# Two transformer blocks on one core: down weights on semaphores of their own, unread products in waits, latent rope queries turned on VectorE, a smaller and later scratch fill

## The chip, the cores and the metric

The program runs on one core of one Trainium2 chip. The metric is the device time of one execution in microseconds (us); lower is better. TensorE multiplies matrices, VectorE and ScalarE work elementwise out of on-chip memory, GpSimd does slow vector work and issues gathers, SyncE only issues transfers. All matrices here are f32; a product of a 128x128 stationary block with 512 columns stands in the trace as two records.

## The reference, cut to what matters

Two blocks of two layers each work on 512 tokens of width 1024. In the first block, each layer has a latent attention (MLA, 8 heads) and a dilated attention:

```python
q = (rms_norm(c_q, q_norm_g) @ w_uq).reshape(B, S, MLA_HEADS, MLA_NOPE + MLA_ROPE)   # 384 -> 8 x (64 + 32)
q_rope = apply_rope(q[..., MLA_NOPE:], cos, sin)
s = (einsum('bqhd,bkhd->bhqk', qn, k_nope) + einsum('bqhr,bkr->bhqk', qr, k_rope)) * scale
```

apply_rope turns a pair of halves: (x1 cos - x2 sin, x1 sin + x2 cos). In the second block each layer ends in a mixture of 16 experts, of which each token takes two:

```python
for wg, wu, wd, cw in experts:          # wg, wu: 1024 x 256; wd: 256 x 1024
    acc += ((silu(t @ wg) * (t @ wu)) @ wd) * cw
```

## The kernel before, in words

There is no scheduler. Each engine has its instructions written out in order (functions marked on("tensor"), on("vector"), ...), and semaphores order the engines.

**Latent queries (first_block).** Events of the projection bank psA are numbered by hand: event n of a layer uses bank n % 2, and TensorE waits in bank_free(n) until event n - 2 has been copied out. PA_VM, PA_KM, PA_QM are the events of the values, the first keys and the first two queries, PA_MLA the first event of each pair of heads. For each head, w_uq holds 128 columns: 64 plain, 32 rope, and the same 32 rope columns with their halves swapped. So project_q makes one head of 128 rows with three products (384 inputs), and queries_out multiplies it by a table (scale, cos, sin) on VectorE. The scores multiply these 128 rows with keys whose rope rows stand twice, which adds the two parts of the rotation. Eight head projections are made per layer: two ahead of the first scores, and two in the second step (t = 1) of each of the pairs j = 0, 1, 2. A step (j, t) is: scores of one tile of queries, values of the step before, a projection, the transposition of the first head's probabilities, for some steps a further projection, the transposition of the second head's.

**Scratch fill.** ys in device memory receives the experts' outputs. GpSimd fills all of it once with finite numbers, at the end of first_block, and waits for it; VectorE waits for ys_filled before it sums the modulation columns.

**Experts (second_block).** Tokens are sorted into 12 runs of up to 128 rows (PARTS, RUNS). A run holds rows of one expert or of parts of two. USES is the order in which the 16 experts' weights are first used, EXP_BUFS = 5 buffers hold gate and up weights (gu_w) and down weights (down_w). SyncE issues the loads in load_experts. load_gate_up(u) waits until the gate product of the run that used the buffer before is done, load_down(u) until the down product of that run is. Both count on one semaphore, exp_loaded of the buffer, and weights(c), which TensorE runs ahead of gate_up(c), waits for 32 on it: for both. TensorE's order is turn_rows(c + 2), turn_hidden(c), gate_up(c + 1), down(c), and so on; the last run has its gate half (last_gate) and its up half (last_up) around down of the run before.

**Unread products.** unread(count) multiplies ones with ones into a bank that nobody reads. Before the change it stands at the program's start and in experts(l).

The parts of the second block that the change also touches: turn_ctx and the key and value projections of the context, route_turned and route (router logits, inside out_product), last_rows and second_rows (the sum of the experts' outputs over the tokens) and project_u (the odd layer's first projection).

## Time and profile before

| | us |
|---|---|
| median of 3 runs | 1970.52 (1969.63 to 1974.61) |
| the profiled execution, its own time | 1959.03 |
| its span | 1957.4 |
| TensorE busy | 1897.8 |
| VectorE, ScalarE, GpSimd busy | 750.1, 546.4, 732.5 |
| mean granted TensorE clock | 0.988 of 2.4 GHz |

Busy is the time in which an engine had an instruction at work. The granted clock is a share of 2.4 GHz; it takes the two levels 1.0 (2.4 GHz) and 0.5 (1.2 GHz), and a value between them is a mean over both. The profiled execution is 11.5 us below the median of the runs.

### The profile page before, as it was taken

What the parts mean: (1) busy time and instruction counts of PE and PEld (TensorE: products, weight loads), DVE (VectorE), ACT (ScalarE), POOL (GpSimd) and SP (SyncE); (2) the same over time, 40 slices, a digit from 0 to 9 for tenths busy, and PEclk for the clock granted to TensorE, in tenths of its full rate; (3) what the DMA queues carried; (4) which work ended last, traced back from release to release, by engine and by line L of the source; (5) the groups of instructions that cost most, each with busy time, mean ns of one, the idle gap of its engine ahead of it and who ended that gap; (6) DMA issues with size and microseconds to landing.
All of it is one profiled execution on the core that took longest, in us unless ns stands there. A gap on an engine that the chain in (4) does not pass through costs nothing.

```text
span 1957.4 us, 25950 instructions
## 1 busy us (share of the span) xinstructions
PE 1897.8 (97%) x9760; PEld 1005.7 (51%) x9760; DVE 750.1 (38%) x1637; ACT 546.4 (28%) x1187; POOL 732.5 (37%) x1065
## 2 busy tenths in 40 slices
PE   8999999999999999999999999999998899999988
PEld 6644556656457455565665455654443344444433
DVE  1343443433221243434336563843532401334424
ACT  3243432214321334422124222742211221012110
POOL 0767676765666667676700012100110100001101
PEclk9999999999999999999999999999999999999999
DMA  7332343244344353333384312042799722047996
GB/s 292 123 109 101 127 148 121 87 144 142 137 169 141 105 199 107 135 138 116 138 335 162 129 38 86 2 181 98 284 366 369 252 91 86 30 186 256 362 377 247
DMA packets 71706, 328.70 MB, mean 168 GB/s; under 512 B 8680, under 2 KB 11174, under 8 KB 56998
## 3 DMA queue, kind: packets, MB, share of 16 engines
q1 hardware_dynamic: 41688, 217.00, 29.9%
q0 software_dynamic: 26736, 98.58, 14.5%
q10 hardware_dynamic: 3168, 11.54, 1.5%
q8 instruction: 79, 1.29, 0.3%
q14 instruction: 35, 0.29, 0.0%
HBM read 288.29 MB, written 38.80 MB: 167 GB/s over the span
## 4 chain that ended last, share of the span: by engine, by line
PE 88%; DMA 5%; DVE 3%; issue 2%; ACT 1%; DVEq 1%; SPq 0%; POOL 0%; ACTq 0%; POOLq 0%
PE psA L464 26%; PE psA L1815 10%; PE psA L456 9%; PE psA L1950 6%; PE psA L1852 6%; PE psA L627 6%; PE psSO L1968 4%; PE psT L443 3%; DMA pool_mem<-in_w_dn 3%; PE psA L505 3%; PE psSO L534 3%; PE psSO L544 2%; DVE pool_mem L2894 1%; PE psSO L565 1%; PE psSO L600 1%
## 5 line engine op out<-in xcount | busy, mean ns | idle before, releaser
L464 PE MATMUL psA<-gB,pool_mem 128*128 128x512 f32 x1024 | 455.3, 597 | 0.0
L395 POOL TENSOR_TENSOR pool_mem<-pool_mem,cs 128x256 f32<-128x256 f32 x448 | 269.3, 634 | 126.4 <-DMA pool_mem<-in_mod_w 125.8
L464 PEld LDWEIGHTS psA<-gB,pool_mem 128*128 128x128 f32 x1024 | 189.5, 190 | 224.2 <-issue 224.2
L399 POOL TENSOR_TENSOR pool_mem<-pool_mem 128x256 f32<-128x256 f32 x336 | 248.1, 766 | 30.9 <-issue 22.9
L1815 PE MATMUL psA<-pool_mem 128*128 128x512 f32 (+1 forms) x528 | 210.7, 558 | 6.0 <-DVE pool_mem L1584 3.4
L456 PE MATMUL psA<-pool_mem,gB 128*128 128x256 f32 (+2 forms) x768 | 190.8, 404 | 1.7 <-ACT gB L797 1.2
L1764 POOL DMA_INDIRECT pool_mem<-xs_scratch,idx x38 | 35.4, 932 | 391.0 <-DVE idx L2568 361.1
L456 PEld LDWEIGHTS psA<-pool_mem,gB 128*128 128x128 f32 x768 | 144.6, 191 | 44.3 <-issue 8.3
L1950 PE MATMUL psA<-pool_mem 128*32 128x512 f32 (+1 forms) x896 | 146.2, 618 | 10.9 <-DMA pool_mem<-in_w_dn 10.9
L1815 PEld LDWEIGHTS psA<-pool_mem 128*128 128x128 f32 x528 | 100.3, 192 | 109.8 <-issue 99.8
L1852 PE MATMUL psA<-pool_mem 128*128 128x512 f32 x256 | 113.9, 595 | 0.8 <-issue 0.8
L627 PE MATMUL psA<-pool_mem 128*128 128x512 f32 x256 | 111.9, 594 | 0.0
L443 PEld LDWEIGHTS psT<-ident,pool_mem 128*128 128x128 f32 x624 | 74.3, 142 | 52.7 <-issue 45.3
L407 POOL DMA_DIRECT2D pool_mem<-in_mod_w x56 | 50.4, 904 | 129.8 <-issue 122.4
L1950 PEld LDWEIGHTS psA<-pool_mem 128*32 128x32 f32 (+1 forms) x896 | 48.6, 125 | 94.0 <-issue 94.0
L996 DVE LOAD_MASK_SELECT pool_mem<-psA x48 | 0.7, 14 | 243.8 <-PE psA L464 243.8
L443 PE MATMUL psT<-ident,pool_mem 128*128 128x128 f32 x624 | 89.0, 275 | 3.7 <-DVE pool_mem L975 1.9
L1968 PE MATMUL psSO<-pool_mem 128*32 128x512 f32 (+2 forms) x496 | 88.9, 609 | 1.0 <-DVE pool_mem L2687 1.0
L852 ACT ACTIVATE pool_mem<-pool_mem,rl 128x512 f32<-128x512 f32 x128 | 84.7, 710 | 7.7 <-DVE rl L1039 7.6
L816 ACT ACTIVATE pool_mem<-psA 128x256 f32<-128x256 f32 x32 | 12.3, 383 | 257.3 <-PE psA L456 257.3
L627 PEld LDWEIGHTS psA<-pool_mem 128*128 128x128 f32 x256 | 47.9, 190 | 58.4 <-issue 56.8
L1852 PEld LDWEIGHTS psA<-pool_mem 128*128 128x128 f32 x256 | 47.1, 190 | 55.0 <-issue 54.7
(345 smaller groups left out, 2371.0 us busy)
## 6 DMA issues: line engine op xcount, KB each, us to landing
pool_mem<-in_w_gu SPq DMA_DIRECT2D x32, 2048.0 KB, 13.8
pool_mem<-in_mod_w POOLq DMA_DIRECT2D x56, 1024.0 KB, 7.8
pool_mem<-in_w_dn SPq DMA_DIRECT2D x32, 1024.0 KB, 12.6
pool_mem<-in_w_qk SPq DMA_DIRECT2D x24, 1024.0 KB, 5.1
ys_scratch<-pool_mem POOLq DMA_DIRECT2D x1, 11264.0 KB, 42.1
ys_scratch<-pool_mem ACTq DMA_DIRECT2D x22, 512.0 KB, 11.5
pool_mem<-in_odd_w_in SPq DMA_DIRECT2D x5, 2048.0 KB, 9.7
pool_mem<-in_w_out SPq DMA_DIRECT2D x4, 2048.0 KB, 8.1
```

The source lines that it names most:

```text
L395: nc.gpsimd.tensor_tensor(wm[:, b, k], wm[:, b, k], c_all[:, k].to_broadcast([P, MCH]), ALU.mult)
L399: nc.gpsimd.tensor_tensor(wm[:, b, k], wm[:, b, k], wm[:, b, n + k], ALU.add)
L443: m = nc.tensor.transpose(psT[:, e % 2, tile(i)], block_in, ident[:])
L456: m = nc.tensor.matmul(psA[:, n % 2, 0:cols], hT[:, k, tile(t)], w[:, k, :], start=(k == 0), stop=(k == KD - 1))
L464: m = nc.tensor.matmul(psA[:, n % 2, :], w(i), src[:, k, :], start=(i == 0), stop=(i == len(ks) - 1))
L505: m = nc.tensor.matmul(psA[32 * t:32 * t + 32, n % 2, 0:2 * P], around(hT_wide[:, k, :])[:, c, t], near_w[:, k, :], start=(k == 0), stop=( ...
L627: m = nc.tensor.matmul(psA[:, half, :], mixT[:, k, tile(t)], width(OUT_SLOT[half], 512)[:, k, :], start=(k == 0), stop=(k == KD - 1))
L852: nc.scalar.activation(prob[:, h, 0:keys], prob[:, h, 0:keys], ACT.Copy, scale=rl[:, h:h + 1]).then_inc(p_normed, 1)
L1815: m = nc.tensor.matmul(psA[:, n % 2, 0:width], lhs, rhs, start=(i == 0), stop=(i == len(pairs) - 1))
L1852: m = nc.tensor.matmul(psA[:, half, :], mixT[:, k, tile(t)], halves[half][0][:, k, :], start=(k == 0), stop=(k == KD - 1))
L1950: m = nc.tensor.matmul(psA[lo:hi, b, :], xgT[:, b, k, lo:hi], gu_w[USES.index(r) % EXP_BUFS][:, k, :], start=(k == 0), stop=(k == KD - 1))
L1968: m = nc.tensor.matmul(psO[lo:hi, half, :], hidT[:, b, k * P + lo:k * P + hi], down_w[USES.index(r) % EXP_BUFS][:, k, half * 512:half * 51 ...
```

## The change

Six edits:

1. **Latent queries.** w_uq has 768 columns: the 64 plain columns of all heads (blocks 0 to 3, two heads each), then the 32 rope columns of all heads (blocks 4 and 5, four heads each). Six projections per layer are made in place of eight. VectorE scales the plain rows into qT (queries_out), and makes the rotation (turning_out): a shuffle that swaps halves, two multiplications by tables, and one addition of 32 rows for each head. qT is set to zero once, since its other 32 rows are now unused. Heads 6 and 7 are put in place later (turning_late).
2. **Order ahead of the first scores.** The rope block, the keys and the first plain block are projected first, the values (PA_VM) last.
3. **Down weights apart.** Gate and up weights count on gate_up_loaded, down weights on down_loaded (three semaphores, taken in turn). gate_up waits for the former, down for the latter. From expert u = 5 on, the load of gate and up is issued ahead of the down load of the expert before it. A down load also waits until the down load three before it has landed.
4. **Unread products** in eight more places of the code, and a larger count in an old one.
5. **Scratch fill.** Only the rows from ROWS[-1] on are filled (11 blocks of 128 in place of 22), by GpSimd behind its pooling work in the second block, from a tile of h. VectorE waits for it in add_output of layer 0.
6. The tables and the weight layout on the host side follow from 1.

```diff
-PA, PA_CKV, PA_V0, PA_VM, PA_KM, PA_QM, PA_GB, PA_OUT = 88, 4, 8, 16, 20, 21, 76, 80
-PA_MLA = (23, 29, 35, 41)
+PA, PA_CKV, PA_V0, PA_QR, PA_KM, PA_QM, PA_VM, PA_GB, PA_OUT = 86, 4, 8, 16, 17, 18, 19, 74, 78
+PA_MLA = (23, 28, 34, 39)
+PA_SECOND = (3, 4, 3)
...
-                load(0, d["w_uq"][L], 3 * 1024)
+                load(0, d["w_uq"][L], 3 * 768)
...
-            pool.wait_ge(const_loaded, 48)
-            ys = d["ys"].rearrange("(c p) n -> p c n", p=P)
-            pool.dma_start(ys, qtab[:].rearrange("p (o h) n -> p o (h n)", o=1).to_broadcast(list(ys.shape))).then_inc(ys_filled, 16)
-            pool.wait_ge(ys_filled, 16)
...
             turn_h(0, 1)
+            unread(6)
             turn_h(0, 2)
...
+                pe.wait_ge(w_loaded[0], 16 * (LOADS[0] * L + 2))
+                project_q(L, 4, PA_QR)
                 pe.wait_ge(spare_loaded, 48 * L + 32)
+                project_k(L, 0, PA_KM)
+                project_q(L, 0, PA_QM)
                 for t in range(NT):
                     n = PA * L + PA_VM + t
...
-                project_k(L, 0, PA_KM)
-                pe.wait_ge(w_loaded[0], 16 * (LOADS[0] * L + 2))
-                for h in range(2):
-                    project_q(L, h, PA_QM + h)
                 pe.wait_ge(*turned_of(TT * L + T_KR))
-                for t in range(NT):
-                    pe.wait_ge(*copied_of(PA * L + PA_VM + t))
...
-                                project_q(L, 2 * j + 2, n + 2)
+                                project_q(L, 5 if j == 1 else j + 1, n + 2)
...
-                            elif t == 1:
-                                project_q(L, 2 * j + 3, n + 3)
+                            elif t == 1 and j == 1:
+                                project_q(L, 2, n + 3)
...
-            def queries_out(L, head, n):
+            def queries_out(L, j, n):
                 n += PA * L
                 dve.wait_ge(pa_ready, n + 1)
-                nc.vector.tensor_tensor(qT[:, (head // 2) % 2, head % 2, :], psA[:, n % 2, :], qtab[:, head % 2, :], ALU.mult)\
-                    .then_inc(pa_copied[n % 2], 1)
+                for h in range(2):
+                    m = nc.vector.tensor_scalar(qT[rows(h), j % 2, h, :], psA[rows(h), n % 2, :], QK_M ** -0.5, None, ALU.mult)
+                m.then_inc(pa_copied[n % 2], 1)
+
+            def turning_out(L, block, n):
+                n += PA * L
+                dve.drain()
+                dve.wait_ge(pa_ready, n + 1)
+                nc.vector.stream_shuffle(swapped[:], psA[:, n % 2, :], MIRROR)
+                nc.vector.tensor_tensor(turning, psA[:, n % 2, :], qtab[:, 0, :], ALU.mult).then_inc(pa_copied[n % 2], 1)
+                dve.drain()
+                nc.vector.tensor_tensor(swapped[:], swapped[:], qtab[:, 1, :], ALU.mult)
+                dve.drain()
+                for head in range(4 * block, 4 * block + (2 if block else 4)):
+                    out, own = turning_rows(head)
+                    nc.vector.tensor_tensor(out, turning[own], swapped[own], ALU.add)
+                if block:
+                    nc.vector.tensor_tensor(turning[rows(1)], turning[rows(1)], swapped[rows(1)], ALU.add)
+                    dve.drain()
...
             def load_down(l, u, e):
                 b = u % EXP_BUFS
                 if u >= EXP_BUFS:
                     sp.wait_ge(yc_half[1], RUNS * l + RUN_OF[USES[u - EXP_BUFS]] + 1)
-                sp.dma_start(down_w[b], rows(d["w_dn"][l][e])).then_inc(exp_loaded[b], 16)
+                if l or u >= DOWN_SEMS:
+                    sp.wait_ge(down_loaded[u % DOWN_SEMS], DOWN_LOADED[u % DOWN_SEMS] * l + 16 * (u // DOWN_SEMS))
+                sp.dma_start(down_w[b], rows(d["w_dn"][l][e])).then_inc(down_loaded[u % DOWN_SEMS], 16)
...
+                behind = None
                 for u in range(EARLY + 1, EXPERTS):
                     e = expert_of(u)
                     load_gate_up(l, u, e)
-                    load_down(l, u, e)
+                    if behind:
+                        load_down(l, *behind)
+                    behind = (u, e)
+                load_down(l, *behind)
...
+            unwritten = d["ys"][ROWS[-1]:, :].rearrange("(c p) n -> p c n", p=P)
+            pool.dma_start(unwritten, h[:, 0:1, :].to_broadcast(list(unwritten.shape))).then_inc(ys_filled, 16)
...
+            def keep_warm(bank, count):
+                for _ in range(count):
+                    nc.tensor.matmul(bank[:, 0:P], ones[:], ones[:], start=True, stop=True)
...
                 route(l, 2)
+                keep_warm(psA[:, 0, :], 3)
                 turn_residual(3, 1)
+                keep_warm(psA[:, 0, :], 5)
                 route_turned(l, 3)
+                keep_warm(psA[:, 0, :], 1)
                 route(l, 3)
...
-                unread((0, 1)[l])
+                unread((2, 1)[l])
...
                 def down(c):
                     b = c % 2
+                    down_weights(c)
...
                 if l == 0:
+                    keep_warm(psA[:, 0, :], 6)
                     second_rows(1)
...
+            keep_warm(psO[:, 1, :], 8)
             pe.wait_ge(t_copied, T_K)
...
             turn_tile(T_ODD, N_ODD, 2)
+            keep_warm(psS[:, 0, :], 5)
             project_u(2)
             turn_tile(T_ODD, N_ODD, 3)
+            keep_warm(psS[:, 0, :], 5)
             project_u(3)
```

How this moves instructions, at three places. First TensorE in layer 0 of the first block, the steps (j = 0, t = 1) and the scores of the next, before (L464 is a projection's product, L443 a transposition, L534 scores, L544 values):

```order
L534 MATMUL psSO<-pool_mem 128x512 x2
L544 MATMUL psSO<-pool_mem 64x128 x8
L464 MATMUL psA<-pool_mem 128x512 x3
L443 MATMUL psT<-ident,pool_mem 128x128 x4
L464 MATMUL psA<-pool_mem 128x512 x3
L443 MATMUL psT<-ident,pool_mem 128x128 x4
```

and now (L532, L542, L462, L441 are the same lines of the changed kernel):

```order
L532 MATMUL psSO<-pool_mem 128x512 x2
L542 MATMUL psSO<-pool_mem 64x128 x8
L462 MATMUL psA<-pool_mem 128x512 x3
L441 MATMUL psT<-ident,pool_mem 128x128 x8
L532 MATMUL psSO<-pool_mem 128x512 x2
```

The second projection between the two transpositions is gone; the same holds for j = 2, and for both layers, four places in all.

Second, SyncE's loads in layer 0 of the experts, from expert u = 4 on, before (L1629 loads gate and up weights, L1635 down weights; an ISA row carries the wait of the load behind it):

```order
L1629 DMA pool_mem<-in_w_gu 128x4096
L1635 ISA
L1635 DMA pool_mem<-in_w_dn 128x2048
L1520 TENSOR_LOAD plan
L1520 ISA x2
L1629 ISA [waits gu_ready]
L1629 DMA pool_mem<-in_w_gu 128x4096
L1635 ISA [waits yc_half1]
L1635 DMA pool_mem<-in_w_dn 128x2048
```

and now (L1660 gate and up, L1668 down):

```order
L1660 DMA pool_mem<-in_w_gu 128x4096
L1551 TENSOR_LOAD plan
L1551 ISA x2
L1660 ISA [waits gu_ready]
L1660 DMA pool_mem<-in_w_gu 128x4096
L1668 ISA [waits down_loaded1]
L1668 DMA pool_mem<-in_w_dn 128x2048
L1551 TENSOR_LOAD plan
L1551 ISA x2
L1660 ISA [waits gu_ready]
L1660 DMA pool_mem<-in_w_gu 128x4096
L1668 ISA [waits down_loaded2,yc_half1]
```

Each down load now stands one place later, behind the gate and up load of the next expert.

Third, TensorE at the end of the router of layer 0 before (L1835 and L1829 are logits, L1542 a transposition, L1878 and L1882 rows of gates that are needed later):

```order
L1835 MATMUL psSO<-pool_mem 128x20
L1542 MATMUL psT<-ident,pool_mem 128x128 x4
L1829 MATMUL psSO<-pool_mem,rtw 32x128 x8
L1835 MATMUL psSO<-pool_mem 128x20
L1878 MATMUL psA<-gB,ones 128x512
```

and now (L1878, L1573, L1872 and L1924 are those lines, L1862 the unread products):

```order
L1878 MATMUL psSO<-pool_mem 128x20
L1862 MATMUL psA<-ones 128x128 x3
L1573 MATMUL psT<-ident,pool_mem 128x128 x4
L1862 MATMUL psA<-ones 128x128 x5
L1872 MATMUL psSO<-pool_mem,rtw 32x128 x8
L1862 MATMUL psA<-ones 128x128
L1878 MATMUL psSO<-pool_mem 128x20
L1924 MATMUL psA<-gB,ones 128x512
```

Nine unread products stand ahead of three instructions that wait for VectorE or ScalarE.

## Rows read from the trace of the kernel before

**Rows 1.** The page's part 1: busy us, share of the span, instructions.

```profile
PE 1897.8 (97%) x9760; PEld 1005.7 (51%) x9760; DVE 750.1 (38%) x1637; ACT 546.4 (28%) x1187; POOL 732.5 (37%) x1065
```

**Rows 2.** TensorE's waits: us in total, times, longest us.

```profile
PE psA L1950 <- DMA pool_mem<-in_w_dn: 10.9, 2, 5.8
PE psA L1986 <- DMA pool_mem<-in_w_dn: 4.8, 2, 2.4
PE psT L1924 <- DMA pool_mem<-xs_scratch,idx: 4.0, 2, 2.8
PE psSO L2072 <- DMA pool_mem<-ys_scratch,slots: 2.5, 1, 2.5
...
PE psA L1815 <- DVE pool_mem L2432: 2.3, 1, 2.3
PE psT L443 <- DVE pool_mem L975: 1.9, 1, 1.9
PE psSO L534 <- DVE pool_mem L1027: 1.8, 2, 0.9
```

**Rows 3.** Timeline of TensorE, step (j = 0, t = 1): start us, us.

```profile
117.67 2.74 PE L464 MATMUL psA<-pool_mem 128*128 128x512 f32 x6
...
120.25 0.60 PE L443 MATMUL psT<-ident,pool_mem 128*128 128x128 f32 x4
```

**Rows 4.** Timeline of VectorE and ScalarE, layer 0 of the first block.

```profile
78.71 2.80 DVE L1107 COPY pool_mem<-psT 64x512 f32<-64x512 f32 x4
...
115.04 1.32 ACT L852 ACTIVATE pool_mem<-pool_mem,rl 128x512 f32<-128x512 f32 x2
...
115.25 3.08 DVE L1127 CAST pool_mem<-pool_mem 128x512 bf16<-128x512 f32 x4
```

**Rows 5.** Timeline of TensorE, last runs of layer 0's experts.

```profile
1492.23 9.17 PE L1950 MATMUL psA<-pool_mem 128*32 128x512 f32 x64 [5.18 <-DMA pool_mem<-in_w_dn]
...
1506.00 7.07 PE L1950 MATMUL psA<-pool_mem 128*32 128x512 f32 x64
...
1520.23 5.34 PE L1968 MATMUL psSO<-pool_mem 128*32 128x512 f32 x32
```

**Rows 6.** The same, layer 1.

```profile
1896.70 10.02 PE L1950 MATMUL psA<-pool_mem 128*32 128x512 f32 x64 [5.77 <-DMA pool_mem<-in_w_dn]
```

**Rows 7.** Stretches: us, TensorE busy (records), granted clock, DMA share, GB/s.

```profile
18.50:22.00 3.50, 3.50 (x11) 0.51 1.05 441
1175.60:1179.10 3.50, 3.50 (x10) 0.51 0.00 0
1363.40:1370.20 6.80, 6.21 (x24) 0.50 0.99 363
1380.40:1387.30 6.90, 6.25 (x14) 0.51 0.48 156
1545.10:1548.60 3.50, 3.50 (x6) 0.63 1.01 399
1405.00:1487.00 82.00, 82.00 (x510) 1.00 0.99 359
1500.00:1510.00 10.00, 10.00 (x98) 1.00 0.73 267
```

**Rows 8.** The chain that ended last: start us, us; transfers of down weights.

```profile
1474.46 17.63 DMA pool_mem<-in_w_dn
...
1506.63 12.46 DMA pool_mem<-in_w_dn
```

**Rows 9.** The page's part 6: transfers, KB each, us to landing.

```profile
pool_mem<-in_w_dn SPq DMA_DIRECT2D x32, 1024.0 KB, 12.6
...
ys_scratch<-pool_mem POOLq DMA_DIRECT2D x1, 11264.0 KB, 42.1
```

**Rows 10.** Timeline: GpSimd's last pooling instruction, VectorE ahead of add_output.

```profile
1231.51 1.27 POOL L1745 TENSOR_TENSOR pool_mem<-pool_mem 128x512 f32<-128x512 f32 x1
...
1295.21 0.18 DVE L2447 TENSOR_TENSOR pool_mem<-ident 128x20 f32<-128x20 f32 x1 [3.81 <-PE psSO L2172]
```

More of the change, by code:

```diff
@@ L121, in first_block @@
     t1, t2 = swapped[:, 0:256], swapped[:, 256:512]
+    turning = at(W_AT + 19200, S)
+    MIRROR = list(range(ROPE_M // 2, ROPE_M)) + list(range(ROPE_M // 2))
     SWAP = list(range(ROT_D // 2, ROT_D)) + list(range(ROT_D // 2)) + list(range(ROT_D, 32))
@@ L510, in project_k, with project_q @@
                 columns(PA * L + n, lambda k: ukv_v[k][:, tile(j)], cT, (3, 4))
-            def project_q(L, head, n):
-                columns(PA * L + n, lambda k: uq_v[:, k, tile(head)], cT, (0, 1, 2))
+            def project_q(L, block, n):
+                columns(PA * L + n, lambda k: uq_v[:, k, tile(block)], cT, (0, 1, 2))
             def project_ga(L, j, n):
@@ L549, in mla_values @@
             def mla_values(L, m):
+                for t in range(NT if m == 0 else 0):
+                    pe.wait_ge(*copied_of(PA * L + PA_VM + t))
                 for h in range(2):
@@ L1022, in dil_turned_out, with turning_rows, turning_late @@
                     .then_inc(turned_copied[e % 2], 1)
-            def queries_out(L, head, n):
+            def queries_out(L, j, n):
                 n += PA * L
                 dve.wait_ge(pa_ready, n + 1)
-                nc.vector.tensor_tensor(qT[:, (head // 2) % 2, head % 2, :], psA[:, n % 2, :], qtab[:, head % 2, :], ALU.mult)\
-                    .then_inc(pa_copied[n % 2], 1)
+                for h in range(2):
+                    m = nc.vector.tensor_scalar(qT[rows(h), j % 2, h, :], psA[rows(h), n % 2, :], QK_M ** -0.5, None, ALU.mult)
+                m.then_inc(pa_copied[n % 2], 1)
+            def turning_rows(head):
+                start = HD * (1 - head % 2)
+                return qT[start:start + ROPE_M, (head // 2) % 2, head % 2, :], slice(ROPE_M * (head % 4), ROPE_M * (head % 4) + ROPE_M)
+            def turning_out(L, block, n):
[13 more added lines that the diff above has]
+                    dve.drain()
+            def turning_late():
+                for head in (6, 7):
+                    out, own = turning_rows(head)
+                    nc.vector.tensor_copy(out, turning[own])
             def gated_out(L, k, gate, n):
@@ L1108, in _ @@
                 m.then_inc(turned_copied[e % 2], 1)
-                for h in range(2):
-                    queries_out(L, h, PA_QM + h)
+                turning_out(L, 0, PA_QR)
+                queries_out(L, 0, PA_QM)
                 for j in range(PAIRS_1):
@@ L1129, in _ @@
                             queries_keys_out(L, 0, j, t // 2)
-                        elif j < 3 and t == 1:
-                            queries_out(L, 2 * j + 2, n + 2)
                         elif j == 3 and t != 2:
@@ L1136, in _ @@
                             rotated(0, j, t // 2)
+                        elif j == 1 and t == 1:
+                            turning_out(L, 1, n + 2)
+                            queries_out(L, 2, n + 3)
                         elif j < 3 and t == 1:
-                            queries_out(L, 2 * j + 3, n + 3)
+                            if j == 2:
+                                turning_late()
+                            queries_out(L, j + 1, n + 2)
                         elif j == 3 and t != 2:
@@ L1276 @@
 MOVES = sum(1 for parts in PARTS for r, _, _, _ in parts if r >= STATIC)
-LOADED = [32 * len(USES[b::EXP_BUFS]) for b in range(EXP_BUFS)]
+LOADED = [16 * len(USES[b::EXP_BUFS]) for b in range(EXP_BUFS)]
+DOWN_SEMS = 3
+DOWN_LOADED = [16 * len(USES[b::DOWN_SEMS]) for b in range(DOWN_SEMS)]
 GATHERED = [16 * sum(len(parts) for parts in PARTS[b::2]) for b in range(2)]
@@ L1460, in second_block @@
     y2_added = sem("y2_added")
+    ys_filled = sem("ys_filled")
     r_ready = sem("r_ready")
@@ L1481, in per_layer @@
         return [sem(f"{name}{l}") for l in range(DEPTH)]
-    exp_loaded = [sem(f"exp_loaded{b}") for b in range(EXP_BUFS)]
+    gate_up_loaded = [sem(f"gate_up_loaded{b}") for b in range(EXP_BUFS)]
+    down_loaded = [sem(f"down_loaded{b}") for b in range(DOWN_SEMS)]
     idx_moved = sem("idx_moved")
@@ L3072, in layouts @@
     out["mask"] = -8 * mask
-    out["q_tab"] = np.stack([np.concatenate([plain, turned]), np.concatenate([turned, plain])], 1).astype(np.float32)
+    out["q_tab"] = np.concatenate([turned] * 4).astype(np.float32)
     return {k: np.ascontiguousarray(v) for k, v in out.items()}
```

50 lines of the change are left out of this document (25 added, 25 removed).

## Prediction

> **What bounds the kernel now.** I read the page's first part, then the table of waits, then the timeline of the stages that the change touches, then the granted clock over short stretches. TensorE is busy for 97% of the span [rows 1], so time can be won in three ways only: less work on TensorE, shorter waits of TensorE, and work that runs at 2.4 instead of 1.2 GHz. The table of waits shows that no single wait is long; the largest are the two for down weights ahead of the gate product L1950 (10.9 us in two waits) and ahead of the last gate product L1986 (4.8 us in two) [rows 2]. The stretches show the third part: in some places the granted clock is 0.50 or 0.51, the lower of its two levels, while TensorE is busy nearly throughout [rows 7]. Work that runs there takes twice as long. A difference of about 0.3% (6 us) is what a measurement of this kernel can tell from no change.
>
> **Edit 1, two projections fewer per layer.** A head's projection is six records, and lasts from 117.67 to 120.25 us, 2.58 us [rows 3]. Two go per layer, over two layers four: 4 x 2.58 = 10.3 us. All of it is on the path, because TensorE had no wait in these steps. Does one come up? In the shortened step, the second transposition moves from 120.25 to about 117.7. It needs the second head's probabilities, which ScalarE finished at 115.04 + 1.32 = 116.36 [rows 4], 1.3 us before. The values of this step need VectorE's copy of the first head's transposition. In layer 0 the mask casts end at 115.25 + 3.08 = 118.3 [rows 4], and that copy (0.7 us) now stands directly behind them, so it ends at 119.0, while TensorE wants it behind the transposition (0.6 us) and the next scores (four records at 0.43): at 117.7 + 0.6 + 1.7 = 120.0. So I charge nothing.
>
> VectorE gets more work. Copies of 64 rows took 2.80 / 4 = 0.70 us each [rows 4], as much as full ones, so the 32-row additions are priced alike. turning_out is then 7 instructions for block 4 and 6 for block 5, some 4.9 and 4.2 us. Block 5 comes at j = 1, t = 1; with the two instructions of queries_out behind it, VectorE comes about 2 us late to the maximum of the next scores. That next step (t = 2) has a full projection of 7 us between scores and transposition, which covers it. If that cover were gone it would cost 2 us per layer. The other end of this price is nothing.
>
> **Edit 2, the order ahead of the first scores.** The first scores waited 0.9 us per layer for the last query to be copied, 1.8 us in total [rows 2]. Four value products (1.7 us each, four records) now stand between that copy and the scores: the wait goes. A smaller one comes: counted from the end of the rope block's projection, turning_out holds VectorE for 4.9 us and the copy of the first plain block needs 1.4 more, 6.3; the keys (1.7), the plain block (2.6) and the first value product (1.7) fill TensorE for 6.0, and the second value product needs that bank. I charge 0.3 us per layer (bounds: nothing, and 1.4 us if all of the copy shows). Edits 1 and 2 together: 10.3 + 1.8 - 0.6 = **11.5 us**.
>
> **Edit 3, down weights apart.** The gate product at 1492.23 had waited 5.18 us and then took 9.17 us, against 7.07 us for the next one of the same shape: 2.1 us more [rows 5], since the wait had brought the clock down. In layer 1 the wait is 5.77 us and the product 10.02 us, 2.95 us more [rows 6]. The last gate product waited 4.8 us in both layers together [rows 2], and the down product behind it took 5.34 us in layer 0 for 32 records, where half of 7.07 is 3.5: 1.8 us [rows 5]. In all 10.9 + 4.8 + 2.1 + 2.95 + 1.8 = 22.5 us.
>
> What stands in its place? The transfers run at 359 GB/s with a share of 0.99 from 1405 to 1487 us [rows 7]: the stage is limited by bandwidth, and a new order makes no bytes go away. But the first gate product to wait (run 9) needs gate and up weights up to u = 12, and waited for the down weights of u = 12, landed at 1474.46 + 17.63 = 1492.1 [rows 8]. In the new order the down loads of u = 11 and 12 stand behind that gate and up load: 2 x 1.05 MB less [rows 9], at 359 GB/s 5.8 us, so it lands at 1486.3. TensorE comes at 1492.23 - 5.18 = 1487.05: no wait, by little. From there to the gate and up weights of u = 15 the queue holds the same bytes as between the two down loads of before, which landed at 1492.1 and 1519.1 [rows 8]: 27 us, and 2.7 us of it lay idle (share 0.73 over 10 us, [rows 7]) because a down load waited for its buffer at the queue's head. So they land between 1486.3 + 27 = 1513.3 and 1510.6. TensorE would reach the last gate product 5.2 + 2.1 us before 1516.7 (1519.1 less a wait of 2.4), at 1509.4. The wait is then 1.2 to 3.9 us; the DMA also has idle time to use around 1400 us, which the new order uses, so it may be nothing. I take 1 us per layer: 22.5 - 2 = **20.5 us**. Down weights are waited for in down(c), 8 us after the gate product begins; a landing that is 5.8 us later than the gate and up weights' is covered. The new wait of a down load for the one three before it is harmless while a load lands in 12.6 us [rows 9], since three loads are issued over two runs, and a run takes 7.07 + 3.5 = 10.6 us or more.
>
> **Edit 4, unread products.** Each has a quarter of the columns of one product of a projection, 2.58 / 3 / 4 = 0.21 us. At each place they are shorter than the wait that they stand in: 6 (1.3 us) in 1.9 us at the start, 8 (1.7) in 2.3 ahead of the context's projection, 2 of full width (1.7) in 2.8 ahead of L1924, 6 (1.3) in 2.5 ahead of L2072 [rows 2]. They cost nothing there; were none covered, all 48 narrow and 2 wide ones would cost 12 us. What they give back is time at the lower level [rows 7]: half of 3.5 us at 18.5 us and again at 1175.6 us, 1.75 us each; at 1380.4 half of 6.25 us, 3.1 us; at 1545.1 (1 - 0.63) x 3.5 = 1.3 us. In the 6.8 us from 1363.4 TensorE is behind VectorE's routing for most of the time, so that I count 1.0 of 3.1 us. Sum **8.9 us**; the bounds are -12 and +11. I take the full value, because each fill lies in the wait just ahead of a slow stretch.
>
> The Trainium skill, "TensorE: Matmul & The Clock Gate", section "Part 1: The HAM clock gate", says that the clock's monitor runs freely and doesn't begin anew with the kernel's work, so that the place of a change of clock shifts from run to run. By that rule a fill may stand where no fall would have come, and a fall come where no fill stands. If half of the 8.9 us were lost so, the sum would be lower by 4.5 us.
>
> **Edit 5, the scratch fill.** 11264 KB landed in 42.1 us [rows 9], hidden under TensorE's work; half of it takes about 21 us. GpSimd can issue it at 1231.51 + 1.27 = 1232.8, and VectorE asks for it at 1295.2 [rows 10]: 62 us later, hidden again. Nothing either way; if it were late, the first output product's bank would wait, 1 us for each us.
>
> **Sum.** 11.5 + 20.5 + 8.9 = 40.9 us off the span of 1957.4, which gives 1916.5, and 1918.1 for that execution's own time of 1959.03. The median of the runs is 11.5 us above it; I take the same difference off it: 1970.5 - 40.9 = 1929.6.
>
> **The rivals.**
> - *The clock falls anyway.* The fills leave waits of 0.2 to 1 us, and short gaps were enough before. Then the 8.9 us are gone: 1938.5. By the skill's rule above, part of this is to be expected. Chance 0.2.
> - *The wait for weights only moves on.* The stage's bandwidth bounds it; at a slightly lower rate than in the profile, the last gate product waits 6 to 8 us per layer and brings the clock down again. Then edit 3 gives about 8 us instead of 20.5: 1942. For it speaks the DMA share of 0.99; against it the 2.7 us that lay idle. Chance 0.17. Both together: 1951, chance 0.06.
> - *More than forecast.* The timed runs are 11.5 us above the profiled one; if that is in the waits for weights, edit 3 takes part of it too: 1920. Chance 0.06.
> - *Slower.* Down loads stand behind a gate and up load that waits for a buffer. If each down load so landed after its down product was due, each of the 11 runs behind the first would wait for one load, 1.05 MB at 359 GB/s = 2.9 us, over two layers 64 us; against 20 us from the other edits it is slower by 44, 2014. It decides from the point at which a down load is issued less than its landing time, 13 us, ahead of its product. Now that is 24 us or more (it may be issued once the run of five experts before is done), so it gets 0.03.
> - *It does nothing,* because the new waits eat up the gains: 1970, chance 0.02.
>
> **How the numbers follow.** The forecast has 0.46, with a range of its own of 1923 to 1936. The range of 1917 to 1948 takes in the first two rivals and the case of a larger gain, and leaves out the double rival, the slower one and no change, with the tails some 0.17. Faster by over 0.3%: all but the last two, 0.95. Within 0.3%: 0.02. Slower: 0.03.
>
> **What the profile of the changed kernel would show.** Edit 1: 24 projection records fewer (four projections of six), and a second transposition directly behind the first at t = 1. Edit 2: no wait of the scores at L534's place. Edit 3: no wait ahead of the gate product of run 9, and one of at most 4 us ahead of the last gate product, now for gate and up weights. Edit 4: a granted clock of 1.00 in the five stretches of rows 7 that show less, and a mean clock near 0.998. Edit 5: one transfer of 5632 KB at about 1233 us. The prediction is wrong if the wait of the last gate product is over 5 us, if the clock still falls at the router, or if a new wait comes in the attention's steps.

## The result, and the profile after

| | before | after |
|---|---|---|
| median of the runs | 1970.52 us | 1943.18 us (1939.83 to 1944.44) |
| ratio after / before | | 0.9852, 95% interval 0.9824 to 0.9881 |
| profiled span (own time) | 1957.4 (1959.03) | 1938.2 (1939.83) |
| mean granted clock | 0.988 | 0.996 |

The kernel is 27.3 us faster by the medians (23 to 35 by the interval of the ratio), where 40.9 was forecast. The profiled execution moved by 19.2 only. The table of TensorE's waits of the changed kernel answers to [rows 2]: us in total, times, longest.

```profile
PE psA L676 <- DVE pool_mem L1028: 6.1, 2, 5.8
PE psT L1970 <- DMA pool_mem<-xs_scratch,idx: 5.0, 3, 2.7
PE psSO L1948 <- DVE pool_mem L2593: 3.9, 2, 2.0
PE psSO L2116 <- issue: 3.7, 1, 3.7
PE psT L441 <- ACT pool_mem L851: 3.2, 2, 2.5
...
PE psSO L2124 <- DMA pool_mem<-ys_scratch,slots: 1.8, 1, 1.8
...
PE psA L454 <- DMA pool_mem<-in_w_v: 0.8, 2, 0.5
```

Both waits for down weights are gone. The first wait, of the value products (L676) for VectorE's copy of the first queries (L1028), is new. The second is an old one (4.0 us before, there L1924). The last line is new too and small here: a projection waits for weights of the values.

The last runs of layer 0's experts, on TensorE's timeline, answer to [rows 5]:

```profile
1484.97 7.07 PE L2001 MATMUL psA<-pool_mem 128*32 128x512 f32 x64
...
1508.13 1.08 PE L2038 MATMUL psA<-pool_mem 128*64 128x256 f32 x8 [0.60 <-DMA pool_mem<-in_w_gu]
1509.14 3.64 PE L2020 MATMUL psSO<-pool_mem 128*32 128x512 f32 x32
```

The gate product takes 7.07 us without a wait (9.17 before), the last gate product waits 0.60, and the down product behind it takes 3.64 (5.34 before). That is edit 3 as forecast. The stretches answer to [rows 7] (us, TensorE, its weight loads, VectorE, ScalarE, GpSimd busy, granted clock, DMA share, GB/s). The three low ones (98.3, 166.6, 1774.2) are all that there are inside the span; the first two are new:

```profile
18.50:22.00 3.50, 3.40 (x16) 2.46 (x17) 0.84 (x3) 2.00 (x7) 0.00 (x0) 1.00 1.04 437
98.30:105.10 6.80, 6.14 (x8) 2.56 (x9) 0.60 (x1) 0.60 (x1) 3.29 (x5) 0.51 0.05 19
166.60:169.90 3.30, 3.20 (x7) 1.92 (x8) 1.94 (x4) 0.66 (x2) 2.28 (x4) 0.51 0.00 0
1175.60:1179.10 3.50, 2.98 (x19) 2.56 (x18) 1.29 (x3) 0.00 (x0) 0.00 (x0) 1.00 0.00 0
1371.90:1382.10 10.20, 8.45 (x39) 4.71 (x38) 5.08 (x16) 1.79 (x3) 2.17 (x2) 1.00 0.54 206
1405.00:1487.00 82.00, 82.00 (x520) 33.38 (x522) 34.67 (x98) 13.63 (x37) 14.08 (x25) 1.00 1.01 378
...
1774.20:1777.50 3.30, 3.30 (x10) 2.14 (x10) 1.37 (x4) 1.50 (x4) 0.85 (x1) 0.50 0.17 68
```

The first scores came later, not earlier: at 107.20 us, before at 100.47. TensorE's timeline, then VectorE's, then GpSimd's, of the same place in layer 0:

```profile
91.32 1.88 PE L676 MATMUL psA<-pool_mem 128*128 128x512 f32 x4
98.95 8.41 PE L676 MATMUL psA<-pool_mem 128*128 128x512 f32 x12 [5.75 <-DVE pool_mem L1028]
107.20 1.88 PE L532 MATMUL psSO<-pool_mem 128*128 128x512 f32 x4
...
88.63 0.69 DVE L1042 TENSOR_TENSOR pool_mem<-pool_mem 128x512 f32<-128x512 f32 x1
89.40 8.19 DVE L1046 TENSOR_TENSOR pool_mem<-pool_mem 32x512 f32<-32x512 f32 x4
97.52 1.38 DVE L1028 TENSOR_SCALAR pool_mem<-psA 64x512 f32<-64x512 f32 x2
...
90.18 4.60 POOL L397 TENSOR_TENSOR pool_mem<-pool_mem,cs 128x256 f32<-128x256 f32 x8
95.02 5.39 POOL L401 TENSOR_TENSOR pool_mem<-pool_mem 128x256 f32<-128x256 f32 x6 [0.24 <-issue]
```

The four 32-row additions of turning_out (L1046) last 8.19 us. The second of them takes 5.23 us; the same four in layer 1, where GpSimd has no elementwise work at that time, take 0.68 us each:

```profile
L1046 DVE TENSOR_TENSOR pool_mem<-pool_mem x1: 5233/5233/5233, 90.1 to 90.1; 32x512 f32<-32x512 f32 x1
...
L1046 DVE TENSOR_TENSOR pool_mem<-pool_mem x4: 678/682/682, 653.8 to 655.9; 32x512 f32<-32x512 f32 x4
```

That addition stands from 90.1 to 95.3, which is GpSimd's burst of eight multiplications (90.18 to 94.78) and the gap behind it. The copy L1028 behind the additions is late, the second value product waits 5.75 us, the clock falls, and the remaining three products take 8.41 us for 12 records, where 12 records at full clock take 5.42 (e4 below). The place at 166.6 us is alike. An addition with both inputs in on-chip memory (L1005) takes 5.06 us under the burst at 158.80, the maxima and exponentials behind it are late, TensorE's transposition waits 2.49 us, and the clock falls:

```profile
158.90 5.06 DVE L1005 TENSOR_TENSOR pool_mem<-pool_mem 128x512 f32<-128x512 f32 x1
...
158.80 4.61 POOL L397 TENSOR_TENSOR pool_mem<-pool_mem,cs 128x256 f32<-128x256 f32 x8
...
166.70 1.11 PE L441 MATMUL psT<-ident,pool_mem 128*128 128x128 f32 x4 [2.49 <-ACT pool_mem L851]
```

**The theories tested.** T1: VectorE's operations with two inputs in on-chip memory are held up by GpSimd's bursts, and edits 1 and 2 put such operations where TensorE waits for them. Rivals: T2, the reordering or the narrow additions cost by themselves; T3, the transfers hold VectorE up; T4, the fills of edit 4 do the harm.

### The profile page after: what moved, and what is told of

It reads as the page before. It is cut to its first block, busy times and chain, and to the rows that moved or that the text cites. A ratio compares the mean times of both kernels' runs of the same rounds, so it can differ in the third digit from the quotient of the medians.

```text
span 1938.2 us, 26187 instructions
## 1 busy us (share of the span) xinstructions
PE 1887.5 (97%) x9836; PEld 1008.9 (52%) x9836; DVE 784.5 (40%) x1672; ACT 546.1 (28%) x1187; POOL 734.9 (38%) x1065
## 4 chain that ended last, share of the span: by engine, by line
PE 85%; DVE 5%; DMA 5%; issue 2%; ACT 1%; DVEq 1%; SPq 0%; POOL 0%; ACTq 0%; POOLq 0%
PE psA L462 23%; PE psA L1854 10%; PE psA L454 9%; PE psA L2001 6%; PE psA L1895 6%; PE psA L627 6%; PE psSO L2020 4%; PE psT L441 3%; PE psA L503 3%; PE psSO L532 3%; DMA pool_mem<-in_w_v 2%; PE psSO L542 2%; DMA pool_mem<-in_w_gu 1%; DVE pool_mem L2951 1%; PE psT L1970 1%
## 5 line engine op out<-in xcount | busy, mean ns | idle before, releaser
L462 PE MATMUL psA<-gB,pool_mem 128*128 128x512 f32 x1024 | 455.3, 597 | 0.0
L462 PEld LDWEIGHTS psA<-gB,pool_mem 128*128 128x128 f32 x1024 | 189.5, 190 | 224.2 <-issue 224.2
L2001 PE MATMUL psA<-pool_mem 128*32 128x512 f32 (+1 forms) x896 | 141.1, 593 | 0.0
L441 PEld LDWEIGHTS psT<-ident,pool_mem 128*128 128x128 f32 x624 | 73.8, 142 | 53.3 <-issue 42.2
L441 PE MATMUL psT<-ident,pool_mem 128*128 128x128 f32 x624 | 88.5, 275 | 5.6 <-ACT pool_mem L851 3.2
```

The lines of the kernel that those rows point to most:

```text
L441: m = nc.tensor.transpose(psT[:, e % 2, tile(i)], block_in, ident[:])
L462: m = nc.tensor.matmul(psA[:, n % 2, :], w(i), src[:, k, :], start=(i == 0), stop=(i == len(ks) - 1))
L2001: m = nc.tensor.matmul(psA[lo:hi, b, :], xgT[:, b, k, lo:hi], gu_w[USES.index(r) % EXP_BUFS][:, k, :], start=(k == 0), stop=(k == KD - 1))
```

## The experiments

The ratios are to the kernel before on the same chip, with 95% intervals. Runs e0 to e3 were compared on one chip, e4 to e6 on a second, e7 to e10 on a third. "Start of X" is the start of the same TensorE product in each trace: A, the first scores (before 100.5, after 107.2); B, the first transposition behind the attention of layer 1 (before 1125.2, after 1128.0); C, the last gate product of layer 0 (before 1519.2, after 1508.1).

### The changed kernel again (e0)

> The changed kernel once more, as the measure for the other three on the same chip and for a question of its own: whether the 3.2 us lost behind the last gate product of layer 1 (TensorE waits 3.71 us at 1922.78 where it waited 0.69 before) comes again. If it belongs to the program (theory: ScalarE's instructions reach it late at that place in this layout), the wait is again above 3 us; if it was chance, it is under 1 us and the span 2 to 3 us shorter. The time against the kernel before: 25 to 30 us less.

Measured: 1941.39 us, ratio 0.9877 (0.9852 to 0.9902); single runs from 1930.4 to 1946.2. A 105.6, B 1126.5, C 1510.0. The wait at the end is there again, 4.29 us, so it belongs to the program. What did not come again is the high clock: this execution has four low stretches inside its span.

```profile
95.40:102.10 6.70, 3.51 (x4) 1.51 (x5) 3.11 (x4) 0.00 (x0) 5.67 (x8) 0.50 0.00 0
1372.00:1382.20 10.20, 9.58 (x24) 5.95 (x25) 4.30 (x13) 1.79 (x3) 2.16 (x2) 0.50 0.51 190
1767.90:1778.10 10.20, 9.52 (x26) 5.87 (x26) 4.35 (x13) 1.19 (x2) 1.88 (x2) 0.50 0.51 182
1924.90:1931.60 6.70, 5.02 (x6) 2.19 (x7) 2.73 (x4) 0.60 (x1) 0.00 (x0) 0.50 0.60 238
```

The products behind the router of layer 0 ran at 1.00 in one execution (39 records in 10.2 us) and at 0.50 in the other (24 records), with the same fills ahead of them. The first trace is the exception: in those of e1, e4, e5, e6, e7 and e9, which have these fills too, the clock is low there as well, for 7.5 to 11 us.

### Edits 1 and 2 undone (e1)

```diff
-PA, ..., PA_QR, PA_KM, PA_QM, PA_VM, ... = 86, ..., 16, 17, 18, 19, ...
+PA, ..., PA_VM, PA_KM, PA_QM, ... = 88, ..., 16, 20, 21, ...
-                project_q(L, 4, PA_QR)
...
+                for h in range(2):
+                    project_q(L, h, PA_QM + h)
```

> The changed kernel with edits 1 and 2 undone (eight latent projections a layer, values projected before keys and queries), the rest kept. By my prediction's sum this is 11.5 us slower than the changed kernel. Theory T1 (the two edits gain where VectorE has its port alone, but in layer 0 VectorE's operations with both inputs in on-chip memory stand still for a whole burst of GpSimd's eight multiplications, 4.6 us, and the value products wait): the first scores come 6.7 us earlier in layer 0, layer 0's TensorE total is equal or 2 us shorter than in the changed kernel up to the end of the latent steps, layer 1's is 4 to 5 us longer, so the whole is -4 to +2 us against the changed kernel. Rival T2 (the lost time is the price of the reordering or of the narrow additions themselves, in both layers): layer 1 would be shorter too and the whole 6 us or more faster than the changed kernel.

Measured: 1942.06 us, 0.9892 (0.987 to 0.9913), against 0.9877 of e0. A 98.5, B 1123.3. The two edits together are worth 3 us with an interval of 6 on either side; 11.5 was forecast. A comes 7.0 us earlier than in e0 and B still 3.2 us earlier: what the edits win between A and B is 3.8 us, nearly all of it behind the first scores of layer 1. That is as T1 expects, and not as T2 does, which had this kernel 6 us or more faster than the changed one.

### Edit 3 alone (e2)

> The kernel before with edit 3 alone (a signal of their own for the down weights and the load order). My prediction's term: 20.5 us less than the kernel before, of which about 9 + 3 us in layer 0 around the last gate product and its down product and 10 us in layer 1. Rival: the bytes are the limit there and the wait only moves to the next product, then 0 to 10 us less. The traces so far speak for 12.8 + 11.3 less some 3 us that went elsewhere: I expect 18 to 24 us less.

Its edit is the part of the diff from DOWN_SEMS to down_weights, applied to the kernel before. Measured: 1938.4 us, 0.9874 (0.9855 to 0.9894): 24.7 us less. The last gate product waits 0.1 us in layer 0 and 0.6 in layer 1. Edit 3 alone gives as much as the whole change does on the same chip (0.9877).

### No fills (e3)

> The changed kernel without edit 4 (no unread products but those that the kernel before has). My prediction's term: 8.9 us more than the changed kernel. By the milestones of the trace the fills gave 1.7 at the start, 1.7 at the context, 1.0 in the router and 2.7 at the gather of layer 0 and 1.6 at the last rows: 8.7 us more. Rival: part of the clock's low stretches stand in waits that VectorE or a DMA ends anyway, as in layer 1's gather, where they cost nothing before; then 3 to 5 us more.

Its edit takes out every keep_warm and the added unread products. Measured: 1932.3 us, 0.984 (0.9817 to 0.9862): 9 us faster than e0 by the medians, 7 by the ratios. Both expectations were wrong in sign. The trace shows it in the attention, A 100.7 and B 1114.6: 4.8 us ahead of e0 at A and 11.9 at B. Of the 7 us between, 2.7 are a wait at the addition under the next burst, which stands for 5.21 us at 157.28 us in e0 and isn't held here, and 2.4 are waits for weights of the values, which e0 has and this trace doesn't. The timeline of VectorE, then of GpSimd, then the single instructions of both (ns: min/median/max):

```profile
90.30 3.82 DVE L1045 TENSOR_TENSOR pool_mem<-pool_mem 32x512 f32<-32x512 f32 x4
...
90.90 5.97 POOL L397 TENSOR_TENSOR pool_mem<-pool_mem,cs 128x256 f32<-128x256 f32 x8
```

```profile
L1045 DVE TENSOR_TENSOR pool_mem<-pool_mem x4: 683/1007/1080, 90.3 to 93.1; 32x512 f32<-32x512 f32 x4
...
L397 POOL TENSOR_TENSOR pool_mem<-pool_mem,cs x4: 621/1056/1080, 90.9 to 93.5; 128x256 f32<-128x256 f32 x4
```

Here the burst began 0.60 us behind VectorE's first addition, 0.08 us before its end; in the changed kernel it began 0.78 us behind, in e0 0.82. The two engines then take turns at some 1.05 us each (0.68 and 0.60 alone), and VectorE needs 3.82 us for the four, not 8.19.

### GpSimd's sums left out, in the kernel after (e4) and before (e4b)

```diff
-                for k in range(KD):
-                    nc.gpsimd.tensor_tensor(wm[:, b, k], wm[:, b, k], c_all[:, k].to_broadcast([P, MCH]), ALU.mult)
-                pool.drain()
-                for n in (4, 2):
...
```

> The changed kernel with GpSimd's multiplications and all but the last addition of the modulation sums left out, so that those sums are wrong and the transfers of their weights stay. T1 (VectorE is held up by GpSimd's bursts on the port that they share): in layer 0 the four additions take 2.8 us as in layer 1, not 8.2; the wait of the value product is 0.3 to 1 us, not 5.75; the clock stays at 1.00; the rotated addition at 158.9 is under 1.1 us; the layer 0 part is 12 to 16 us shorter. Rival T3 (the transfers into on-chip memory, not GpSimd, hold VectorE up): the additions stay at about 8 us and the wait above 5 us.

> The kernel before with the same part of GpSimd's work left out (modulation sums wrong). T1: the kernel before has fewer two-input operations on the path, so it gains less than the changed kernel does: 2 to 6 us against 12 to 16. Rival T2 (edits 1 and 2 cost by themselves): both gain alike and the distance between the two quiet kernels stays at about 27 us. By T1 that distance grows to 35 to 40 us, near the forecast 40.9.

Measured: 2134.35 us (1.0843) and 2169.26 us (1.103). Without these parts the sums come out otherwise, the tokens go to other experts, and behind the last run of layer 0's experts (1512 us in e4) both kernels spend over 200 us more than their full versions, much of it in the experts' overflow; only what lies ahead can be compared. The additions of e4 (L1039 there), and its value products on the timeline:

```profile
L1039 DVE TENSOR_TENSOR pool_mem<-pool_mem x4: 678/682/683, 88.7 to 90.7; 32x512 f32<-32x512 f32 x4
```

```profile
92.78 5.42 PE L669 MATMUL psA<-pool_mem 128*128 128x512 f32 x12 [0.32 <-DVE pool_mem L1021]
```

B is 1111.9 in e4 and 1123.2 in e4b. So the changed kernel reaches B 14.6 us earlier without GpSimd's sums (against e0) and the kernel before 2.0. These 2.0 stand already at 26.8 us, 1.7 of them in the low stretch at the start, which e4b's trace doesn't have. With the transfers still there and the sums gone the stall is gone: T3 falls. Without GpSimd's sums, edits 1 and 2 are worth 1123.2 - 1111.9 = 11.3 us (up to 25 us the two traces agree to 0.1 us, so that the start fill has no part in it), and 11.5 was forecast: T2 falls too.

### ScalarE scales the first queries (e5)

```diff
                 keys_out(L, 0, PA_KM)
+                queries_scaled(L, 0, PA_QM)
...
                 turning_out(L, 0, PA_QR)
-                queries_out(L, 0, PA_QM)
+                dve.drain()
+                dve.sem_inc(kr_ready, 1)
```

queries_scaled is two ScalarE copies with scale=QK_M ** -0.5; the first scores wait for kr_ready once more.

> The changed kernel, where the first pair's latent queries are scaled out of their bank by ScalarE (two copies, some 0.6 us each) and no longer by VectorE behind the turned additions; the first scores wait for the additions. T1: the additions are as slow as before (8.2 us in layer 0), but nothing waits for them until the first scores: the value product's wait in layer 0 falls from 5.75 to under 1.5 us and the clock does not fall, so the first scores come 6 to 9 us earlier than 107.2 and the kernel is 6 to 9 us faster than the changed one. Rival: the scores then wait for the additions instead, which end at 97.6 us, or ScalarE's value copies are later by 1.2 us and hold the value products: 0 to 3 us faster.

Measured: 1931.33 us, 0.9811 (0.9785 to 0.9836): 8 to 13 us faster than the changed kernel (0.9852, 0.9877). VectorE's additions, ScalarE's copies and TensorE:

```profile
89.08 8.21 DVE L1056 TENSOR_TENSOR pool_mem<-pool_mem 32x512 f32<-32x512 f32 x4
...
91.21 1.19 ACT L837 ACTIVATE pool_mem<-psA 64x512 f32<-64x512 f32 x2 [1.38 <-PE psA L462]
...
91.01 7.03 PE L678 MATMUL psA<-pool_mem 128*128 128x512 f32 x16
97.87 1.88 PE L534 MATMUL psSO<-pool_mem 128*128 128x512 f32 x4
```

The additions are as slow as ever and nothing waits for them: they end at 97.3, and the scores come at 97.87. A is 7.7 us ahead of e0. The interval of the ratio overlaps that of the changed kernel's first measurement (from 0.9824) and not that of e0 (from 0.9852).

### A pause in GpSimd's bursts (e6)

```diff
                 for k in range(KD):
                     nc.gpsimd.tensor_tensor(wm[:, b, k], ..., ALU.mult)
+                    if k % 2:
+                        pool.drain()
```

(and the same among the additions.)

> The changed kernel with a drain behind every second of GpSimd's multiplications and additions, so that its burst of eight (4.60 us) is cut in pieces of about 1.2 us. T1, with VectorE let in whenever GpSimd pauses: the longest stall of a VectorE operation with two on-chip inputs falls from 5.1 to 1.2 to 2 us, the value product's wait from 5.75 to 1 to 3 us, and the kernel gets 4 to 10 us faster. Rival: drains do not let VectorE in (or GpSimd's own work gets so late that VectorE waits for the modulation sums at about 1031 us, where there are 40 us in hand): no change or slower.

Measured: 2010.71 us, 1.0229 (1.0202 to 1.0256), slower. Both theories had a part: A comes at 100.3 with a wait of 2.1 us, but GpSimd is late with its sums, and VectorE behind it.

```profile
PE psSO L602 <- DVE pool_mem L1023: 76.8, 1, 76.8
```

The 40 us that I thought to have in hand were far too few for this many drains.

### The start fill alone taken out (e7)

> The changed kernel without the six unread products of the start alone (the other fills kept). T1 in its sharper form (what decides is when VectorE's additions begin against GpSimd's burst: in the changed kernel the second addition meets a burst that has begun at 90.18 us and waits it out, without the fills the additions begin at 90.3, ahead of the burst at 90.9, and it is GpSimd that waits): the four additions take 3.8 us in place of 8.2, the value product waits 1.4 us in place of 5.75, the clock does not fall, the addition at about 158 us is not held, and the kernel is 8 to 12 us faster than the changed one although 1.1 to 1.7 us of the start come back. Rival T4 (the 9 us by which the kernel without any fill was faster come from the fills in the router, where the product then waits 1.96 us for VectorE and the clock falls again behind it): equal to the changed kernel or up to 2 us slower.

Measured: 1934.88 us, 0.986 (0.9842 to 0.9878), not to be told from the changed kernel. The sharper form of T1 missed: the value product waited 5.9 us as in e0, and A is 105.7. In this execution the clock did not fall at 18.5 us although no fill stood there, so nothing moved against the burst (additions from 88.95, burst from 89.78, 0.83 us behind). The start fill is not what decides, then; what e3 gained at A came with an execution that reached this place about 1 us later. How often that happens isn't shown: there is one trace for each kernel. The time is what T4 expected of this run; T4 is tested by the next two.

### On the version of e5: without the router's fills (e8), without any (e10)

```diff
-                keep_warm(psA[:, 0, :], 3)
                 turn_residual(3, 1)
-                keep_warm(psA[:, 0, :], 5)
                 route_turned(l, 3)
-                keep_warm(psA[:, 0, :], 1)
```

> The kernel in which ScalarE scales the first pair's queries, without the nine unread products in the router of each layer. T4: the router's fills hold the clock for 1 us and then the product waits for VectorE and the clock falls anyway, so that without them the kernel is 2 to 6 us faster than with them (1926 to 1929). My prediction's term (1.0 us in layer 0) would make it 1 to 2 us slower (1932 to 1933).

> The kernel in which ScalarE scales the first pair's queries, without any of edit 4's fills: here the additions are off the path, so the fills' own worth shows. My prediction's term: 8.9 us slower than with them (1940). By the milestones of the trace without fills the start gives 1.1, the context 1.1, the last rows 1.7 and the gather of layer 0 and the router nothing or a loss: 0 to 4 us slower (1931 to 1935).

Measured: e8 1926.95 us, 0.9814 (0.9802 to 0.9827), equal to e5 by the ratio; its median is lower because all kernels were some 4 us faster on this chip, the kernel before too (1963.25 against 1967.65). e10 1928.85 us, 0.9837 (0.9819 to 0.9855), 5 us slower by the ratio, with intervals that overlap. So T4 falls: neither version is faster for lack of fills. The router's fills give nothing that shows. All fills together give about 5 us or less, where 8.9 was forecast, and that isn't told from nothing: from B to the end the traces of e0, e1, e5, e7 and the changed kernel, with all fills behind B, take 810.2 to 818.2 us, and those of e2, e3 and e10, without any, 811.2 to 816.4.

### The loads in their old order (e9)

```diff
-                    if behind:
-                        load_down(l, *behind)
-                    behind = (u, e)
-                load_down(l, *behind)
+                    load_down(l, u, e)
```

> The changed kernel with the signals apart but the old order of the loads (gate and up weights of an expert, then its down weights). If the separate signal is what pays (a gate product no longer waits for the down weights of its own expert, which take about 2.9 us of the transfers' time), it keeps 8 to 10 us of layer 0's and of layer 1's gain and is 0 to 3 us slower than the changed kernel. If the order is what pays, the late gate products wait 2 to 3 us more each, at two places a layer: 6 to 12 us slower.

Measured: 1954.01 us, 0.9944 (0.9923 to 0.9966): 13 us slower than e0. That is the second expectation's side, just over its 6 to 12. C comes 7.8 us later than in e0:

```profile
1492.48 8.77 PE L1997 MATMUL psA<-pool_mem 128*32 128x512 f32 x64 [2.82 <-DMA pool_mem<-in_w_gu]
...
1517.79 1.08 PE L2034 MATMUL psA<-pool_mem 128*64 128x256 f32 x8 [1.06 <-DMA pool_mem<-in_w_gu]
```

With the signal alone a gate product waits for its own gate and up weights, which stand behind an earlier expert's down weights. The gate product of run 9 waits 2.82 us in layer 0 and 3.6 in layer 1 (5.18 and 5.77 before), and each wait still brings the clock down (8.77 against 7.07). About half of edit 3 is the order.

## Why the prediction was right, and where not

The measured time lies inside the range of 1917 to 1948 and outside the forecast's own 1923 to 1936. It is near the 1942 of the rival "The wait for weights only moves on", by chance: that mechanism did not come. Two of the prediction's own signs of being wrong did: new waits in the attention's steps, and a clock that still falls at the router.

- **Edit 3**, forecast 20.5, measured 24.7 (interval 21 to 28) by e2. The mechanism was right: no wait ahead of run 9's gate product, the down product at full clock, down weights never waited for. The term "I take 1 us per layer" for the last gate product was a little too large, 0.60 and nothing. The wait of 0.60 us is below the 1.2 us at which the sum's landing times began.
- **Edits 1 and 2**, forecast 11.5, measured 3 (plus or minus 6) by e1. The step that failed is the one on the bank of the second value product: "I charge 0.3 us per layer (bounds: nothing, and 1.4 us if all of the copy shows)". In layer 1 it holds, 0.32 us. In layer 0 it was 5.75 us and a fall of the clock. The price of 0.70 us for a narrow addition came from copies out of a product's bank (psT) [rows 4], which have one input only; the additions read two tensors in on-chip memory while GpSimd multiplies. The trace of before held the warning: GpSimd is 37% busy [rows 1], and I never looked at what it does to VectorE. With GpSimd's sums left out the two edits' term is right to 0.2 us (e4, e4b), and with the copy moved to ScalarE most of the loss at A is had back (e5). From A to B, the shortened steps are worth 10.9 us without GpSimd's sums, as priced (10.3 and a little of edit 2), but only 4.0 in the changed kernel and 3.8 in e0 against e1. The sum had no term for additions that stood there before and now meet another burst: the one at 158.9 us cost 2.5 us of wait and a fall of the clock in the changed kernel, 2.7 us of wait in e0, and nothing in e4. Nor had it one for the waits for the values' weights, 0.8 and 2.4 us in these two traces and none before; what makes these weights late wasn't looked for.
- **Edit 4**, forecast 8.9, measured 5 or less (e5 against e10), and in the changed kernel the fills could not be told from a loss (e3). The step that failed is "I take the full value, because each fill lies in the wait just ahead of a slow stretch". At three places the clock did not fall in any trace that has the fill: at the start, ahead of the context's projection, and at the gather of layer 0 (e4 and e4b, whose experts run otherwise, are left out of this last one). But without the fill it doesn't always fall there. At the start it fell in three of six traces (before, e2 and e3, not e4b, e7 and e10), ahead of the context's projection in four of five (not e3), and at the gather in three of four (not e2). Behind the router of layer 0 the fills did not hold it: it fell in seven of the eight traces that have them, in e0 for 10.2 us. There the product behind them waits 1.97 us for VectorE (L1948), which it did not before. The rule of the Trainium skill that the prediction quoted, from "TensorE: Matmul & The Clock Gate", section "Part 1: The HAM clock gate", that the place of a change of clock shifts from run to run, agrees with e0 and the changed kernel's first trace. How much it comes to only the traces tell: 33.8 and 13.4 us of low clock in one and the same program.
- **Edit 5**: one transfer of 5632 KB, issued at 1233.8 us and landed after 18.3, and no wait for it, as forecast. No run takes the edit alone.
- **Not forecast:** ahead of the last rows of layer 1, TensorE waits for ScalarE's copy of the combination weights. It waited 0.69 us before, 3.7 after, and 2.9 to 4.3 in every other kernel here that has edit 3 (e9 too, so the order of the loads isn't it), apart from e4, whose experts run otherwise. In nine of them (not in the changed kernel's first trace and e8) the eight records of the last rows behind the wait take 5.2 to 6.7 us in place of 3.70, at a lower clock. TensorE had turned them 3.0 us earlier (1918.41 and 0.66 long); ScalarE had been idle for 12.07 us, and the timeline names no releaser of this program:

```profile
1909.67 0.39 ACT L2349 ACTIVATE pool_mem<-psA 128x256 f32<-128x256 f32 x1 [10.75 <-PE psA L2038]
1922.12 0.60 ACT L2385 ACTIVATE pool_mem<-psT 128x512 f32<-128x512 f32 x1 [12.07 <-remote]
```

  Between the two stands the branch around the overflow. Why ScalarE comes out of it late stays open; no run was spent on it.

The forecast of 1930 so missed by 13 us: about 8.5 too much for edits 1 and 2, 4 or more for edit 4 and 3 for the end of layer 1, against 4 too little for edit 3. Each of these shares has an interval of some us, so that the sum closes only roughly. The kernel with e5's and e8's edits has the lowest median of all that were run, 1926.95 us, 0.9814 of the kernel before (e5: 0.9811). That it ends close to the number that was forecast is no proof of the forecast: it gets there by a copy that the change doesn't have.

## What to carry to other kernels

Before an operation with two inputs in on-chip memory is put on VectorE ahead of something that TensorE waits for, look at what GpSimd does at that time, and price it from a row of the same operand places, not of the same size. If it can't be moved, keep what the next product needs (here the copy that frees a bank) off the engine that may be held up. Loads that are limited by bandwidth are worth ordering by when each part is needed, and a fill that keeps the clock up is to be judged over several executions, since a single trace may show a fall that the next one doesn't have.

## What the runs showed of the hardware

- VectorE and GpSimd, each with inputs in on-chip memory, meet in two ways. In e3 GpSimd's burst began 0.08 us before the end of VectorE's first addition, and they took turns: 1.0 to 1.1 us each, in place of 0.68 and 0.60. In seven other traces (the changed kernel, e0, e5, e7, e8, e9, e10) it began between 0.03 us before that end and 0.15 us behind it, and the next addition stood for all eight multiplications, 5.11 to 5.28 us, and ended behind GpSimd's gap of 0.24 us. So 0.05 us lie between the two; why they differ isn't shown. The Trainium skill, "SBUF — State Buffer", section "Who interferes with whom", says that a VectorE instruction with two such inputs contends with a GpSimd instruction that reads on-chip memory, and that the second to issue blocks until the first has finished. The turns in e3 agree with that. The long stall does not: it lasts over eight instructions, and in six of these seven traces the record of the addition that stood begins some 0.1 us before that of the first multiplication.
- The same program had its clock low for 13.4 us in one execution and for 33.8 us in another. Two of the places are common (near 98 and 1774 us), the one at 166.6 us is in the first trace alone, those at 1372 and 1925 us in the second. Its time varied from 1930.4 to 1946.2 us in six executions.
